# A dense layer in plain fp32 in place of three rounded products, in a two-layer decoder kernel

## What is computed

```
D_MODEL = 1024
SEQ = 256
D_FF = 2816

def dense_swiglu(h, w_in, w_out):
    g, u = jnp.split(h @ w_in, 2, axis=-1)
    return (jax.nn.silu(g) * u) @ w_out

h = layer_norm(ALPHA * h + mix, ln_g[l, 0], ln_b[l, 0])
ffn = dense_swiglu(h, dense_w_in[0], dense_w_out[0])
h = layer_norm(ALPHA * h + ffn, ln_g[l, 1], ln_b[l, 1])
```

## Time and profile before

| | |
|---|---|
| median of 3 runs | 1339.75 us (1337.9 to 1342.03) |
| the profiled execution | 1337.99 us, its span 1336.2 us |
| TensorE (PE) matmul busy | 1309.3 us, 98% of the span |
| VectorE (DVE), ScalarE (ACT), GpSimd (POOL) busy | 396.5, 281.2, 75.8 us |
| dense layer, first matmul to the first transpose after it | 170.93 to 355.33 us of the span |
| expert phase | from 453 us to the end |

### The profile page before, as it was taken

The page is one execution under the profiler, slowest core; times in us unless marked ns, Lnnn a source line. Parts: engine busy times, 40 slices in busy tenths (PEclk is TensorE's granted clock), DMA queues, the critical chain, the costliest instruction groups (busy, mean ns, idle before and its releaser), DMA issues.

```text
span 1336.2 us, 31629 instructions
## 1 busy us (share of the span) xinstructions
PE 1309.3 (98%) x14086; PEld 721.6 (54%) x14086; DVE 396.5 (30%) x681; ACT 281.2 (21%) x510; POOL 75.8 (6%) x104
## 2 busy tenths in 40 slices
PE   9998999999999999999999999999999999999996
PEld 6765788888776534533633543443453363354344
DVE  6569666664676411010101101101101010120222
ACT  5456465553455200000010010000000001000001
POOL 2033200000022200000000000000000000000100
PEclk9999999999999999999999999999999999999999
DMA  9680358955542999999999999999999999999992
GB/s 324 196 220 33 126 192 326 332 189 191 158 140 96 379 397 421 417 399 420 418 398 420 419 402 398 419 418 394 420 417 372 420 418 392 408 419 417 418 420 103
DMA packets 115774, 443.16 MB, mean 332 GB/s; under 512 B 11936, under 2 KB 49088, under 8 KB 101312
## 3 DMA queue, kind: packets, MB, share of 16 engines
q1 hardware_dynamic: 108704, 423.39, 81.7%
q10 hardware_dynamic: 5792, 13.63, 2.8%
q0 software_dynamic: 1152, 4.19, 0.8%
HBM read 425.85 MB, written 15.34 MB: 330 GB/s over the span
## 4 chain that ended last, share of the span: by engine, by line
PE 93%; DVE 3%; ACT 2%; SPq 1%; issue 1%; DMA 0%; DVEq 0%; ACTq 0%
PE bank L1731 43%; PE bank L1724 22%; PE bank L1586 6%; PE bank L1142 4%; PE bank L1144 4%; PE bank L1143 4%; PE bank L1589 3%; PE bank L1159 1%; PE bank L1463 1%; PE bank L1424 1%; ACT arena L948 1%; PE bank L1332 1%; PE bank L1172 1%; DMA ring<-in_w_in_a_dram 0%; ACT wh L770 0%
## 5 line engine op out<-in xcount | busy, mean ns | idle before, releaser
L1731 PE MATMUL bank<-ring,arena 128*32 128x448 f32 x2880 | 275.0, 539 | 0.0
L2226 DVE TENSOR_TENSOR arena<-arena,bank 128x448 f32<-128x448 f32 x48 | 26.9, 617 | 727.8 <-PE bank L1731 727.8
L1731 PEld LDWEIGHTS bank<-ring,arena 128*32 128x32 f32 x2880 | 93.4, 110 | 173.9 <-issue 172.6
L1772 DVE TENSOR_TENSOR wl<-ring,wh 128x2048 fp32r<-128x2048 f32 (+1 forms) x54 | 121.7, 2259 | 55.4 <-ACT wh L770 55.1
L1724 PE MATMUL bank<-ring,arena 128*32 128x256 f32 x2304 | 125.8, 379 | 0.0
L1586 PE MATMUL bank<-hT,wh 128*128 128x512 f32 x344 | 121.6, 399 | 0.0
L770 ACT ACTIVATE wh<-ring 128x2048 fp32r<-128x2048 f32 (+1 forms) x56 | 105.5, 1888 | 37.7 <-PE bank L1144 30.7
L1731 PE MATMUL bank<-wls,arena 128*32 128x448 f32 x1152 | 111.2, 539 | 0.0
L1731 PE MATMUL bank<-whs,arena 128*32 128x448 f32 x1152 | 111.2, 539 | 0.0
L1088 ACT ACTIVATE arena<-bank 128x448 f32<-128x448 f32 x48 | 22.6, 544 | 388.8 <-PE bank L1731 388.8
L1724 PEld LDWEIGHTS bank<-ring,arena 128*32 128x32 f32 x2304 | 74.9, 110 | 52.0 <-issue 3.9
(11 more groups left out here) (293 smaller groups left out, 1294.6 us busy)
## 6 DMA issues: line engine op xcount, KB each, us to landing
ring<-in_moe_w_in_dram SPq DMA_DIRECT2D x120, 896.0 KB
ring<-in_moe_w_out_dram SPq DMA_DIRECT2D x48, 1024.0 KB
whs<-in_moe_w_in_dram SPq DMA_DIRECT2D x48, 896.0 KB, 17.9
wls<-in_moe_w_in_dram SPq DMA_DIRECT2D x48, 896.0 KB, 18.1
arena<-in_moe_w_in_dram SPq DMA_DIRECT2D x32, 896.0 KB, 16.0
whs<-in_moe_w_out_dram SPq DMA_DIRECT2D x24, 1024.0 KB, 21.3
wls<-in_moe_w_out_dram SPq DMA_DIRECT2D x24, 1024.0 KB, 22.3
ring<-in_dense_w_in_dram SPq DMA_DIRECT2D x22, 1024.0 KB
```

The lines of the kernel that those rows point to most:

```text
L1731: ins = pe.matmul(bank[s + GROUPS * (kind == "u")][32 * j:32 * j + 32, 0:BLOCK], xgT[:, c, 32 * s:32 * s + 32], slot[:, BLOCK * j:BLOCK * ...
L1772: dve.tensor_tensor(wl[:, n % SPLITS, 0:size], slot_of(n)[:, 0:size], wh[:, n % SPLITS, 0:size].bitcast(F32), ALU.subtract).then_inc(split, 1)
L2226: ins = dve.tensor_tensor(act[:, s, :], act[:, s, :], bank[GROUPS + s][:, 0:BLOCK], ALU.mult)
```

## The change

The items of the dense layer become whole: no split of them on ScalarE or VectorE, and their slots are reloaded when used. The tokens are copied turned, in fp32, into `hTf` (three copies on ScalarE, one on VectorE). Every product is one plain fp32 matmul with a 128 x 128 stationary operand. Chunk c uses banks 0 and 1 if c is even, 2 and 3 if odd, gate in the first and up in the second, with both column halves in one bank. ScalarE takes the silu straight from the gate's bank, VectorE multiplies straight with the up's bank into `act_dense`. `lower_h` and `move_low` stay for the second normalization alone.

```diff
 def whole(n):
-    return n < N_FIRST and ITEMS[n][0] == "cmp"
+    return n < N_FIRST and ITEMS[n][0] in ("cmp", "dense_in", "dense_out")
...
+            def turn_plain(q, tt):
+
+                act_e.wait_ge(turned, T_H1 + 2 * tt + q + 1)
+                act_e.activation(hTf[:, 4 * q:4 * q + 4, tt * P:tt * P + P],
+                                 bank[TBANK[T_H1 + 2 * tt + q]][:, :].rearrange("p (c n) -> p c n", c=4), ACT.Copy)\
+                     .then_inc(moved_a, 1)
...
+            for c in range(N_DENSE):
+                act_e.wait_ge(used, AT["dense_in"] + 2 * c + 1)
+                if c >= 2:
+                    act_e.wait_ge(act_ready, c - 1)
+                act_e.activation(silu[:, c % 2, :], bank[2 * (c % 2)][:, :], ACT.Silu).then_inc(silu_ready, 1)
...
-            keep_warm(7, 1)
-            lower_h(0, T_H1)
-            keep_warm(7, 7)
+            keep_warm(7, 8)
...
             for c in range(N_DENSE):
                 for gu in range(2):
-                    if c >= 1:
-                        pe.wait_ge((gate_summed, up_summed)[gu], c)
                     n = AT["dense_in"] + 2 * c + gu
+                    if c >= 2:
+                        pe.wait_ge((silu_ready, act_ready)[gu], c - 1)
                     ready(n)
-                    wts = both(n, DC)
+                    wts = slot_of(n).rearrange("p (c n) -> p c n", c=DC)
                     for j in range(2):
...
                         for k in range(DC):
-                            pe.matmul(bank[2 * gu + j], wts[0][:, k, P * j:P * j + P],
-                                      hT[:, k, :, :].rearrange("p a n -> p (a n)"), start=(k == 0), stop=False,
-                                      skip_group_check=True)
-                            ins = pe.matmul(rest, wts[1][:, k, P * j:P * j + P], hTh[:, k, :], start=False,
-                                            stop=(k == DC - 1), skip_group_check=True)
+                            if n == AT["dense_in"] and j == 0 and k % 4 == 0:
+                                moved(pe, T_H1 + k // 4)
+                                moved(pe, T_H1 + 2 + k // 4)
+                            ins = pe.matmul(bank[2 * (c % 2) + gu][:, SEQ * j:SEQ * j + SEQ], wts[:, k, P * j:P * j + P], hTf[:, k, :],
+                                            start=(j == 0 and k == 0), stop=(j == 1 and k == DC - 1), skip_group_check=True)
                     ins.then_inc(used, 1)
...
                 for half in range(2):
                     for j in range(2):
-                        ins = product(bank[4 + 2 * half + tt][:, :],
-                                      [t[:, 2 * c + j, tt * P:tt * P + P] for t in (actTh, actTl)],
-                                      [t[:, j, 512 * half:512 * half + 512] for t in wts],
-                                      False, (c == N_DENSE - 1 and j == 1))
+                        ins = pe.matmul(bank[4 + 2 * half + tt][:, :], act_dense[:, 2 * c + j, tt * P:tt * P + P],
+                                        wts[:, j, 512 * half:512 * half + 512], start=False,
+                                        stop=(c == N_DENSE - 1 and j == 1), skip_group_check=True)
...
+            for c in range(N_DENSE):
+                dve.wait_ge(silu_ready, c + 1)
+                dve.wait_ge(used, AT["dense_in"] + 2 * c + 2)
+                dve.tensor_tensor(act_dense[:, 2 * c:2 * c + 2, :], silu[:, c % 2, :].rearrange("p (a n) -> p a n", a=2),
+                                  bank[2 * (c % 2) + 1][:, :].rearrange("p (a n) -> p a n", a=2), ALU.mult).then_inc(act_ready, 1)
```

More of the change, by code:

```diff
@@ L543, in decoder_kernel @@
         MOVER[late_b[0]], MOVER[late_b[1]] = "av"
-        for first, banks, movers in ((T_X, (4, 5, 6, 7), "vvvv"), (T_H1, (4, 5, 6, 7), "aavv"),
+        for first, banks, movers in ((T_X, (4, 5, 6, 7), "vvvv"), (T_H1, (4, 5, 6, 7), "aaav"),
                                      (T_H2, (0, 1, 4, 6), "aavv"), (T_H3, (4, 5, 6, 7), "aavv")):
@@ L971, in preload, with move_low @@
                      .then_inc(preloaded, 1)
-            def move_low(first, k):
+            def move_low(first):
                 for q in range(2):
-                    act_e.wait_ge(lowered, 2 * k + q + 1)
+                    act_e.wait_ge(lowered, q + 1)
                     act_e.activation(hTl[:, 4 * q:4 * q + 4, 0:P],
@@ L1004, in norm_part @@
                         act_e.activation(pre[:, 0, cols], pre[:, 0, cols], ACT.Copy, scale=std[:, 0, 1:2]).then_inc(pre_scaled, 1)
-                if k < 2:
+                if k == 0:
+                    for q in range(2):
+                        turn_plain(q, 0)
+                elif k == 1:
                     turn_h(first, 0)
@@ L1017, in norm_part @@
                     load_norm(k + 1)
[L1018 to L1021, removed]
+                elif k == 0:
+                    turn_plain(0, 1)
+                    act_e.wait_ge(h_ready, 4)
+                    load_norm(k + 1)
+                elif k == 1:
+                    move_low(first)
+                    split_weights(AT["q_b"] + 2)
                     turn_h(first, 1)
@@ new lines, in _ @@
+            for c in range(N_DENSE):
[3 more added lines that the diff above has]
+                act_e.activation(silu[:, c % 2, :], bank[2 * (c % 2)][:, :], ACT.Silu).then_inc(silu_ready, 1)
+                if c == 2:
+                    moved(act_e, T_H1 + 3)
+                    for half in range(2):
+                        for tt in range(NT):
+                            preload(4 + 2 * half + tt, tt, half)
+                if c == 3:
+                    act_e.wait_ge(zeros_ready, 1)
+                    for half in range(2):
+                        act_e.dma_start(xb.rearrange("(s p) n -> p s n", p=P)[:, :, 512 * half:512 * half + 512],
+                                        zeros.rearrange("p (s n) -> p s n", s=1).to_broadcast([P, GROUPS * NE * CAP // P, 512]))\
+                             .then_inc(zero_filled, 16)
@@ L1515, in next_h, with lower_h @@
                     ins.then_inc(turned, 1)
-            def lower_h(k, first):
+            def lower_h(first):
                 pe.wait_ge(nident_ready, 1)
                 for q in range(2):
-                    pe.wait_ge(high, 4 * (k + 1) + q + 1)
+                    pe.wait_ge(high, 4 + q + 1)
                     pe.matmul(bank[TBANK[first + q]][:, :].rearrange("p (c n) -> p c n", c=4), nident[:, :],
@@ L1598, in _ @@
                     ready(n)
[L1599 to L1600 removed]
+                    pe.wait_ge(act_ready, c + 1)
+                wts = slot_of(n).rearrange("p (c n) -> p c n", c=2)
                 for half in range(2):
                     for j in range(2):
[L1603 to L1606 removed]
+                        ins = pe.matmul(bank[4 + 2 * half + tt][:, :], act_dense[:, 2 * c + j, tt * P:tt * P + P],
+                                        wts[:, j, 512 * half:512 * half + 512], start=False,
+                                        stop=(c == N_DENSE - 1 and j == 1), skip_group_check=True)
                     if tt == NT - 1 and half == 1:
@@ L1612, in _ @@
             keep_warm(3, 1)
-            lower_h(1, T_H2)
+            lower_h(T_H2)
             out_banks_free(0, len(PROJ_A))
@@ L2111, in norm @@
                     scale(k, tt)
-                if k < 2:
+                if k == 0:
+                    dve.wait_ge(turned, first + 4)
+                    dve.tensor_copy(hTf[:, 4:8, P:2 * P], bank[TBANK[first + 3]][:, :].rearrange("p (c n) -> p c n", c=4))\
+                       .then_inc(moved_v, 1)
+                elif k == 1:
                     turn_h(first)
@@ L2117, in _ @@
             norm(0, ((0, 1), (2, 3)), 0, AT["out_a"] + 3, T_H1, (1,))
[L2118 to L2136, removed]
-                    dve.wait_ge(silu_ready, c + 1)
-                    dve.wait_ge(up_summed, c + 1)
-                    dve.tensor_tensor(gated, gated, up, ALU.mult).then_inc(act_ready, 1)
+            for c in range(N_DENSE):
[3 more added lines that the diff above has]
+                                  bank[2 * (c % 2) + 1][:, :].rearrange("p (a n) -> p a n", a=2), ALU.mult).then_inc(act_ready, 1)
             norm(1, ((4, 5), (6, 7)), 2, AT["dense_out"] + N_DENSE - 1, T_H2, (0, 1))
```

25 lines of the change are left out of this document (1 added, 24 removed).

## The result

The changed kernel takes 1381.18 us, the median of 3 runs (1381.17 to 1382.85), against 1339.75 before: a ratio of 1.031, with a 95% interval of 1.028 to 1.034. It is slower by 41.4 us; 1383 was forecast, with a range of 1378 to 1398.

What follows compares the result with a forecast made beforehand. TensorE, busy 98% of the span, was taken as the bound. dense_in +27.4 us and dense_out +15.6 gave +43.1: span 1336.2 to 1379.3, execution 1381.1, with 1.76 to the median 1383 us; range 1378 to 1398.

Steps and rivals of the forecast that it cites:

- The price of a plain matmul: Dense layer: 431.7 ns for 256 moving columns, 858 ns for 512, from a line through the expert phase's matmuls.
- Two records a matmul: Dense layer: each plain fp32 matmul is two records, so 704 in dense_in and 176 in dense_out.
- Rival 2: Dense layer: a full-width plain matmul takes two column times, not four; -70.6 us, 1269 us; chance 4%.
- The splits were worth nothing: Dense layer: splitting on VectorE and ScalarE hides behind the matmuls, so removing it gives nothing by itself.
- The upper bound: Dense layer: plain matmuls drag 10.6% like the rounded pairs, making the layer 249.3 us, +64.9.
- The row between: L1332, two matmuls side by side: 450 ns at full width, making the layer 237.6 us, +53.
- rows 7: Expert-phase chain pieces L1724 and L1731, quarter-width plain matmuls: 36.26 us and 72.16 us, used to price plain matmuls.
- rival 1: Dense layer: whole-tile loads drag on plain matmuls; +53 to +65 us, 1393 to 1405 us; chance 22%.
- One aside: dense_in: the second set of banks covers silu and product, 1.3 us x 11, about 14 us if gone.
- The start of the layer: Before the dense layer: fewer lowering matmuls, splits and changed copies shift nothing; 0, within 0.5 us.
- The ring: Weight slots in the layer: freed after 6.9 us of matmuls, with 48 us of work ahead; priced at nothing.
- the expert phase giving nothing back: After the layer: everything stays as before, only later; its DMA slots are already full, so no time returns.

Runs made afterwards that it cites:

- Experiment 2: Changed kernel with each whole 128x128 matmul of dense_in replaced by four side by side with 32 stationary columns each: 1382.33 us, ratio 1.0323.
- experiment 4: Kernel before without rounding and subtracting the dense layer's 33 items, multiplying stale split buffers: 1339.71 us, ratio 1.0006.
- 5: Changed kernel with rounding and subtracting of all 33 dense items put back, results unread in the layer: 1382.14 us in one execution.
- 6: Kernel before with stationary operands of 64 columns in place of 128 in dense_in's pairs: 1338.01 us in one execution.
- experiment 8: Changed kernel with stationary operands of 64 columns in dense_in, half of the output left out: 1381.9 us in one execution.
- Experiment 1: Changed kernel with one set of banks, gate always bank 0 and up always bank 1: 1381.29 us, ratio 1.0317.
- 7: Kernel before with no splits of the dense items and 64-column stationary operands in dense_in: 1334.86 us in one execution.

## Why the prediction was right

- **The price of a plain matmul** was the step that decided, and it held: 431.7 ns forecast, 151.95 us / 352 = 431.7 ns measured; 858 ns forecast for 512 columns, 75.53 us / 88 = 858.3 ns measured. The line through 256 and 448 columns at quarter width was right for whole ones and beyond its upper end, at 512. Experiment 2 shows why: the width makes no difference.
- **Two records a matmul.** 704 and 176 came. The Trainium skill's two statements ("FP8 and Floating Point Precision": four passes; "Perfetto Trace Analysis": half the rate for FP32_LOW_HIGH) both agree with the trace if the halved rate is that of one record: 213 ns of stream for 256 columns, twice. Rival 2 took it for the whole matmul, and falls.
- **The splits were worth nothing**: shown in the kernel before (experiment 4, ratio 1.0006) and beside plain matmuls (5).
- **The upper bound was a real effect in the wrong place.** The rounded pairs do drag by 10%; 13 of the 34 ns go with half of the load (6), the other 20 or so are open. I had the choice between it and the expert rows and took the latter since the load per record was the same; experiment 8 shows that a plain record does not feel its load. Room to hide the load is not the whole difference: a rounded matmul of 512 columns in dense_out streams for 213 ns beside a whole load, as a plain record of 256 columns does, and takes 227 ns where that takes 216.
- **The row between was read too high.** L1332's 450 ns divide a whole chain piece, with its first load, by 8. In the trace of before, sets of two of its records start 216 ns apart from the second set on, so a matmul of full width costs about 431 ns there, as at rows 7. The lower end of rival 1, +53 us, had no row behind it. Likewise the 108 ns of the 64-column records are an average with a short first one; from the second on their starts lie 112 ns apart.
- **One aside was wrong, without a weight in the sum**: that the second set of banks covers some 14 us. Experiment 1 took it away and lost nothing. I had counted silu and product as exposed in each chunk; but with one set the wait of gate c + 1 is for the silu of c, which ends 0.7 us into the up group of c. The waits should have been laid out against the order first.
- **The start of the layer** was put at 0 within 0.5 us. From the first transposes after the mixing to the first dense matmul it took 5.02 us before (165.91 to 170.93) and 5.15 in the changed kernel (167.62 to 172.77): +0.13. As priced, the two lowering matmuls (0.90 us) gave nothing back: TensorE waits 0.80 us there now for the second normalized tile.

```profile
171.18 1.32 PE L1502 MATMUL bank<-ident,h 128*128 128x128 f32 x8 [0.80 <-DVE h L2057]
```

- **The ring, and the expert phase giving nothing back**: the list of waits has none of TensorE in the changed kernel's layer, and the time after it is equal to 0.02 us.

The forecast lay 1.8 us above the measured median. The term for it is the way from the profiled execution to the median: 1339.75 lay 1.76 us above before's profiled execution, and I carried this over; two of three executions of the changed kernel lie at the 1381.1 that the sum itself gave.

No kernel here that computes the whole result beats the one before; the half-load kernels of experiments 6 and 7, which are faster by 3 and 5 us, leave half of dense_in's output out. Three rounded products need three column times, 3.2 to 3.3 with their drag (680 ns for 213 in dense_out, 354 for 107 in dense_in), a plain product four: in this layer the rounded ones stay ahead by 43 us as long as the splitting engines keep up, and the earlier trace rows show that they do.

## What to carry to other kernels

Before replacing split, rounded products by plain fp32 ones, count column times on TensorE: 3 (here 3.2 to 3.3 with drag) against 4. By this count the plain form can pay only where TensorE waits for the splits, or where the moving operand is so short that the loads set the pace and two of them are fewer than three; no run here shows either case. Work taken from engines that were waiting for TensorE was worth nothing here. And price a matmul form by a chain piece divided by the number of matmuls in the code, not by records or busy time: the busy time of a plain record here is 379 ns, its hold on the array 216.

## What the runs showed that was not expected

**Loads drag on rounded pairs and not on plain matmuls.** A rounded pair holds the array 10% longer than its columns (353 ns for 320), 6% with half loads. Plain matmuls of the same loads lose 1% (431.7 ns for 426.7) and do not change with half of the load. VectorE and ScalarE splitting beside them slow neither form (experiments 5 and 7).

**The first 45 us of an execution differ by up to 5 us.** In experiment 4 the first weights came later than in the profiled execution of before (22.63 us against 20.20, by their chains), and TensorE's granted clock fell in the stretch that follows. The window of before, of the kernel without splits, and of the one with half loads, whose program is up to the layer that of before:

```profile
20.00:45.00 25.00, 24.18 (x115) 19.89 (x114) 18.35 (x43) 15.11 (x21) 1.10 (x1) 1.00 1.00 334
```

```profile
20.00:45.00 25.00, 21.51 (x91) 17.45 (x90) 16.18 (x38) 11.91 (x18) 0.00 (x0) 0.86 1.05 353
```

```profile
20.00:45.00 25.00, 21.71 (x97) 17.69 (x97) 17.36 (x42) 11.90 (x18) 0.00 (x0) 0.93 1.05 354
```

Clock 0.86 and 0.93 are means over full speed and its half, 1.2 GHz, after TensorE had waited for the weights (busy for 21.51 and 21.71 of the 25 us); in before the same stretch has 1.00 and 24.18 us. Their layers started 5.1 and 3.9 us later (176.06 and 174.82 against 170.93). A difference of a few microseconds between single executions of this kernel says nothing of an edit in the layer; the pieces of the chain inside it do: in five kernels with plain dense_in and dense_out they are 151.95 to 152.09 us and 75.53 to 75.73 us.
